# A decoder step on one core: work units dealt anew over the expert groups, ScalarE copies of the late projection, and column-group products in the samples' attention

## What is computed

```
h = x + W_out[ rms(NSA(n)) ; rms(ShortConv(n)) ],  n = rmsnorm(x)
h = h + PEER(rmsnorm(h))
y = h + sigmoid(rmsnorm(h) W_g) * (p W_p)
```

## Time and profile before

| | |
|---|---|
| median of 3 runs | 2665.53 us (2664.52 to 2675.07) |
| the profiled execution's own time | 2674.7 us |
| its span, first to last instruction | 2672.9 us |
| PE, DVE, POOL, ACT busy | 64%, 43%, 34%, 12% of the span |
| mean granted TensorE clock | 0.77 of full speed |
| moved by DMA | 907 MB, mean 339 GB/s |
| of it by the gathers' queue | 671 MB |

### The profile page before, as it was taken

One profiled execution on the slowest core, in us unless ns is written; L12 is line 12 of the kernel. 1 busy time (PEld: TensorE's weight loads), 2 busy tenths in 40 slices (PEclk: granted clock), 3 DMA queues, 4 the chain that ended last, 5 costly groups with the idle time before them and its releaser, 6 DMA issues.

```text
span 2672.9 us, 21406 instructions
## 1 busy us (share of the span) xinstructions
PE 1716.8 (64%) x8331; PEld 935.6 (35%) x8331; DVE 1147.8 (43%) x2124; ACT 331.3 (12%) x711; POOL 921.8 (34%) x644
## 2 busy tenths in 40 slices
PE   7599898998879467677678533332332323477776
PEld 3245576398767346543257300000000000122224
DVE  1001213105442773244543366656556665644442
ACT  1000123001000232120010010100101012001002
POOL 0000000003222452243343256656656655645430
PEclk9799896998889777678878766666565665777888
DMA  9673352768989797689899899999999999999996
GB/s 314 211 280 119 127 175 95 251 213 326 387 333 386 316 387 286 265 316 366 347 417 394 347 418 422 421 421 422 422 422 421 422 422 418 402 416 416 416 418 221
DMA packets 228650, 907.12 MB, mean 339 GB/s; under 512 B 29750, under 2 KB 54198, under 8 KB 144615
## 3 DMA queue, kind: packets, MB, share of 16 engines
q0 software_dynamic: 92160, 671.13, 60.9%
q1 hardware_dynamic: 136174, 233.79, 25.3%
q10 hardware_dynamic: 216, 0.86, 0.1%
HBM read 893.70 MB, written 14.52 MB: 340 GB/s over the span
## 4 chain that ended last, share of the span: by engine, by line
DMA 49%; PE 39%; DVE 4%; issue 2%; ACT 2%; POOL 2%; SPq 1%; DVEq 0%; ACTq 0%; PEldq 0%; POOLq 0%
DMA arena<-in_peer_v,arena 33%; PE bank L1660 8%; DMA arena<-in_w_in 6%; PE bank L2035 5%; PE bank L2052 4%; DMA arena<-in_w_out 3%; DMA arena<-in_peer_wq 3%; PE bank L1724 3%; DMA arena<-in_peer_u,arena 2%; PE bank L1852 2%; PE bank L1828 2%; PE bank L1985 2%; DVE arena L1457 2%; PE bank L2154 2%; DMA arena<-in_state_win 2%
## 5 line engine op out<-in xcount | busy, mean ns | idle before, releaser
L1457 DVE CUSTOM_DVE_ANT_0 arena<-arena 128x2048 f32<-128x2048 f32 x320 | 730.8, 2292 | 623.2 <-DMA arena<-in_peer_u,arena 619.7
L2035 PE MATMUL bank<-arena 128*32 128x512 f32 x2560 | 459.8, 830 | 673.8 <-DVE arena L1466 511.9
L658 POOL DMA_INDIRECT arena<-in_peer_u,arena x320 | 561.1, 1753 | 900.9 <-DVEq L1436 634.0
L663 POOL DMA_INDIRECT arena<-in_peer_v,arena x320 | 360.4, 1126 | 769.0 <-PE bank L2035 739.5
L2035 PEld LDWEIGHTS bank<-arena 128*32 128x32 f32 x2560 | 68.7, 128 | 1019.0 <-DVE arena L1466 516.8
L1660 PE MATMUL bank<-arena 128*128 128x512 f32 (+2 forms) x544 | 219.0, 563 | 37.8 <-DMA arena<-in_w_in 32.4
L2052 PE MATMUL bank<-arena 128*128 128x192 f32 x1024 | 193.4, 353 | 21.1 <-DMA arena<-in_w_in 19.7
L2052 PEld LDWEIGHTS bank<-arena 128*128 128x128 f32 x1024 | 184.9, 208 | 42.2 <-DMA arena<-in_w_in 25.2
L1660 PEld LDWEIGHTS bank<-arena 128*128 128x128 f32 (+1 forms) x544 | 102.7, 210 | 151.0 <-issue 117.6
L954 ACT ACTIVATE arena<-arena 128x4 f32<-128x4 f32 x80 | 16.7, 209 | 974.2 <-DVE arena L1457 974.1
L2154 PE MATMUL bank<-arena 128*128 128x512 f32 x256 | 120.2, 627 | 0.0
(11 more groups left out here) (245 smaller groups left out, 1528.1 us busy)
## 6 DMA issues: line engine op xcount, KB each, us to landing
arena<-in_w_in SPq DMA_DIRECT2D x22, 2048.0 KB, 13.3
arena<-in_w_in SPq DMA_DIRECT2D x32, 1024.0 KB, 14.6
arena<-in_w_out SPq DMA_DIRECT2D x8, 2048.0 KB, 8.2
arena<-in_peer_wq SPq DMA_DIRECT2D x8, 2048.0 KB, 8.0
arena<-in_w_out SPq DMA_DIRECT2D x16, 1024.0 KB, 16.3
arena<-in_peer_wq SPq DMA_DIRECT2D x16, 1024.0 KB, 22.9
arena<-in_ple_gate SPq DMA_DIRECT2D x32, 512.0 KB, 14.6
arena<-in_ple_gate SPq DMA_DIRECT2D x6, 2048.0 KB, 12.7
```

The costliest lines, as they stand in the source:

```text
L658: pool.indirect_dma_start(u_row[j], None, I["peer_u"][0], bass.IndirectOffsetOnAxis(idx[:, i, c + j:c + j + 1], 0)).then_inc(u_in[j], 16)
L663: pool.indirect_dma_start(v_row[j], None, I["peer_v"][0], bass.IndirectOffsetOnAxis(idx[:, i, c + j:c + j + 1], 0)).then_inc(v_in[j], 16)
L1457: dve.tensor_tensor_reduce(out=u_row[j], in0=u_row[j], in1=rep_of(i), scale=1.0, scalar=0.0, op0=ALU.mult, op1=ALU.add, accum_out=a4[:, pa ...
L2035: ins = pe.matmul(bank[i % 2][32 * q:32 * q + 32, :], diag[:, k % 2, j, :], v_row[j][:, 512 * q:512 * q + 512], start=(s == 0 and j == 0), ...
```

## The change

Four edits.

1. **Blocks h are copied like the others.** ScalarE's `late_out` copies h0 and h1 out of PSUM to a place that `h_hold` gives (for h0 the one that b1 uses later, so b1's copy waits for `ch_ev` 1). The next block waits for `cz_ev` alone. VectorE reads the copies. `late_conv` goes to groups 4 and 7, `conv_norm` to 8, `scale_conv` to 9, and ScalarE's and TensorE's parts with them; `conv_sums` is now at the start of group 8's items.
2. **The items are dealt anew**: groups 8, 9 and 10 take items 0-2, 3-5 and 6-8; groups 11 to 15 one each, 9 to 13; group 16 takes 14, 15 and 16; from 17 on as before.
3. **Score products of the samples** go round the four pairs: the same 28 products, each next one for another 32 partitions. `sample_scores(s)` no longer waits for the copy of the pair before last.
4. **Value products of the samples** keep 32 columns of probabilities stationary and stream 128 columns of values, round the same four groups of partitions of bank 3; ScalarE copies the 128x128 result (`sample_rows_out`), TensorE turns it once (`sample_turn`, behind the next pair's scores), and ScalarE copies it to its place. The next `value_load` waits for the products (`ov_mm`), not for the turn.

The diff, cut to its core:

```diff
@@ -173,6 +173,11 @@
     u_rows = buf(ZC0, 512)
+    def h_hold(j, x):
+        return (buf(Z0 + 3584, 4, 192)[:, x, 0:128], buf(Z0 + 3584, 4, 192)[:, x, 128:192]) if j else (conv_P(4 + x), conv_S(4 + x))
@@ -272,7 +277,9 @@
         if k < 8:
             return ()
-        return (2 * (k - 8), 2 * (k - 8) + 1) if k < 16 else (k,)
+        if k < 11:
+            return tuple(range(3 * (k - 8), 3 * (k - 8) + 3))
+        return (k - 2,) if k < 16 else (14, 15, 16) if k == 16 else (k,)
@@ -538,7 +545,10 @@
         def value_load(s):
-            sp.wait_ge(o_mm, 16 + s)
+            if s:
+                sp.wait_ge(ov_mm, s)
+            else:
+                sp.wait_ge(o_mm, 16)
@@ -844,11 +854,15 @@
+        def sample_rows_out(s):
+            act.wait_ge(ov_mm, s + 1)
+            act.activation(pT[:, 1, 0:128], bank[3][:, 0:128], ACT.Copy).then_inc(ov_ev, 1)
+
         def sample_o(s):
             act.wait_ge(o_mm, 16 + s + 1)
             for bb in range(2):
                 ins = act.activation(attT[:, :, (2 * s + bb) * NT:(2 * s + bb) * NT + NT],
-                                     bank[7][:, 384 + 64 * bb:448 + 64 * bb].rearrange("p (h t) -> p h t", h=NH), ACT.Copy)
+                                     bank[3][:, 128 + 64 * bb:192 + 64 * bb].rearrange("p (h t) -> p h t", h=NH), ACT.Copy)
@@ -886,9 +900,11 @@
             if 11 <= k < 15:
                 sample_pt(k - 11)
-                sample_o(k - 11)
+                sample_rows_out(k - 11)
             if 9 <= k < 13:
                 sample_keys(k - 9)
+            if 11 <= k < 15:
+                sample_o(k - 11)
@@ -969,9 +985,9 @@
             kind, j = LATE[b]
-            if kind == "h":
-                return
             act.wait_ge(rc_used, 4 * b + 4)
+            if kind == "b" and j:
+                act.wait_ge(ch_ev, 1)
@@ -985,9 +1001,10 @@
-                elif kind == "b":
-                    act.activation(conv_P(c), src_P, ACT.Copy)
-                    ins = act.activation(conv_S(c), src_S, ACT.Copy)
+                elif kind in "bh":
+                    dst_P, dst_S = h_hold(j, s) if kind == "h" else (conv_P(c), conv_S(c))
+                    act.activation(dst_P, src_P, ACT.Copy)
+                    ins = act.activation(dst_S, src_S, ACT.Copy)
@@ -1009,19 +1026,19 @@
-            if k == 4:
+            if k == 5:
                 u_rows_out(0)
             if k < 7:
                 late_out(k + 1)
-            if k == 6:
+            if k == 7:
                 act.wait_ge(cv_done, 2)
...
                 ins.then_inc(sqc_ready, 1)
-            if k == 7:
+                u_rows_out(1)
+            if k == 8:
                 root(stats[:, 244:246], stats[:, 246:248])
-                u_rows_out(1)
@@ -1532,14 +1549,14 @@
-            dve.wait_ge(cz_ev, 4 if j == 0 else 6)
+            dve.wait_ge(cz_ev, 5 if j == 0 else 8)
...
-            dve.wait_ge(rc_used, 20 if j == 0 else 32)
             for x in range(4):
-                for u, src in ((u_ext[:, x, 2:130], bank[4 + x][:, 0:128]),
-                               (by_sample(u_ext[:, x, 130:210], NT + 2)[:, :, 2:NT + 2], by_sample(bank[4 + x][:, 128:192], NT))):
+                h_P, h_S = h_hold(j, x)
+                for u, src in ((u_ext[:, x, 2:130], h_P),
+                               (by_sample(u_ext[:, x, 130:210], NT + 2)[:, :, 2:NT + 2], by_sample(h_S, NT))):
@@ -1577,8 +1594,8 @@
-        late = {1: head_norm, 2: lambda: scale_heads(0), 3: lambda: (scale_heads(1), late_conv(0)),
-                6: lambda: late_conv(1), 7: conv_norm, 8: scale_conv}
+        late = {1: head_norm, 2: lambda: scale_heads(0), 3: lambda: scale_heads(1), 4: lambda: late_conv(0),
+                7: lambda: late_conv(1), 8: conv_norm, 9: scale_conv}
@@ -1872,7 +1889,8 @@
-            pe.wait_ge(o_ev, 16 + max(0, s - 1))
+            if s == 0:
+                pe.wait_ge(o_ev, 16)
@@ -1883,20 +1901,20 @@
+            groups = [(2 * s + bb, bb, g, 64 * bb + 32 * g,
+                       qsT[:, 2 * s + bb, HPG * g:HPG * g + HPG, :].rearrange("p h t -> p (h t)")) for bb in range(2) for g in range(NG)]
+            for br in range(2):
+                for a in range(2):
+                    for b, bb, g, p0, q in groups:
+                        pe.matmul(bank[4 + br][p0:p0 + 32, 128 * a:128 * a + 128], q, pastT[:, bb, br, a, g, :],
+                                  start=True, stop=True)
...
@@ -1914,21 +1932,24 @@
-                r = slice(64 * bb + 32 * g, 64 * bb + 32 * g + 32)
-                    o = bank[7][:, 384 + r.start:384 + r.stop]
-                    for w in range(2):
-                        for k in range(2):
-                            pe.matmul(o, past_vals[:, w, bb, k, g * HD:g * HD + HD],
-                                      pT[:, 0, 256 * w + 128 * k + r.start:256 * w + 128 * k + r.stop],
-                                      start=(w == 0 and k == 0), stop=False)
...
-            ins.then_inc(o_mm, 1)
+            for w in range(2):
+                for k in range(2):
+                    for bb, g, r in groups:
+                        pe.matmul(bank[3][r, 0:HD], pT[:, 0, 256 * w + 128 * k + r.start:256 * w + 128 * k + r.stop],
+                                  past_vals[:, w, bb, k, g * HD:g * HD + HD], start=(w == 0 and k == 0), stop=False)
...
+            ins.then_inc(ov_mm, 1)
+
+        def sample_turn(s):
+            pe.wait_ge(ov_ev, s + 1)
+            pe.transpose(bank[3][:, 128:256], pT[:, 1, 0:128], ident).then_inc(o_mm, 1)
@@ -1997,6 +2018,8 @@
             if 9 <= k < 13:
                 sample_scores(k - 9)
+            if 11 <= k < 15:
+                sample_turn(k - 11)
@@ -2042,10 +2065,8 @@
-                elif LATE[b - 1][0] == "h":
-                    pe.wait_ge(ch_ev, LATE[b - 1][1] + 1)
                 else:
-                    pe.wait_ge(cz_ev, sum(kind != "h" for kind, _ in LATE[0:b]))
+                    pe.wait_ge(cz_ev, b)
@@ -2091,7 +2112,7 @@
-                4: lambda: u_turn(0), 7: lambda: (u_turn(1), conv_sums())}
+                5: lambda: u_turn(0)}
@@ -2106,6 +2127,9 @@
             if k == 8:
+                u_turn(1)
+                conv_sums()
+            if k == 9:
                 pe.wait_ge(roots_set, 2)
                 root_rows(bank[2], 0, 246, 247).then_inc(roots_mm, 1)
```

More of the change, by code:

```diff
@@ L232, in build @@
     rb_in = [sem(f"rb_in{j}") for j in range(4)]
-    half_ev = sem("half_ev")
+    half_ev, ov_mm, ov_ev = sem("half_ev"), sem("ov_mm"), sem("ov_ev")
     gs_mm = sem("gs_mm")
@@ L1049, in _ @@
                     spread_staged(k // SSTEP + 1)
-            if k < 8:
+            if k < 9:
                 late_behind(k)
@@ L1885, in sample_scores @@
             pe.wait_ge(biased, 16 + s)
-            for bb in range(2):
-                b = 2 * s + bb
-                for g in range(NG):
-                    p0 = 64 * bb + 32 * g
-                    q = qsT[:, b, HPG * g:HPG * g + HPG, :].rearrange("p h t -> p (h t)")
-                    for br in range(2):
-                        for a in range(2):
-                            pe.matmul(bank[4 + br][p0:p0 + 32, 128 * a:128 * a + 128], q, pastT[:, bb, br, a, g, :],
-                                      start=True, stop=True)
-                        pe.matmul(bank[4 + br][p0:p0 + 32, 256:264], q, qkT[:, 8 + 2 * br + g, 256 + b * NT:256 + b * NT + NT],
-                                  start=True, stop=True)
-                    sg = 2 * (1 + b) + g
-                    ins = pe.matmul(bank[4][p0:p0 + 32, 264:264 + NWIN], q, kcT[:, sg * NWIN:sg * NWIN + NWIN],
-                                    start=True, stop=True)
+            groups = [(2 * s + bb, bb, g, 64 * bb + 32 * g,
[4 more added lines that the diff above has]
+                        pe.matmul(bank[4 + br][p0:p0 + 32, 128 * a:128 * a + 128], q, pastT[:, bb, br, a, g, :],
+                                  start=True, stop=True)
+                for b, bb, g, p0, q in groups:
+                    pe.matmul(bank[4 + br][p0:p0 + 32, 256:264], q, qkT[:, 8 + 2 * br + g, 256 + b * NT:256 + b * NT + NT],
+                              start=True, stop=True)
+            for b, bb, g, p0, q in groups:
+                sg = 2 * (1 + b) + g
+                ins = pe.matmul(bank[4][p0:p0 + 32, 264:264 + NWIN], q, kcT[:, sg * NWIN:sg * NWIN + NWIN],
+                                start=True, stop=True)
             ins.then_inc(s_mm, 1)
```

14 lines of the change are left out of this document (7 added, 7 removed).

## The result

The changed kernel took **2629.74 us** (median of 4 runs, 2622.26 to 2634.76), the kernel before, beside it, 2667.73 us: ratio 0.9851, interval 0.9819 to 0.9884. So it is 1.5 to 1.7% faster, 38 to 47 us; forecast were 62, in a range that holds the result.

A forecast was written before the change was run, and what follows sets the result against it. The DMA engines bound the kernel, full from group 28; only their earlier idle time can be won. Gains of 22 (groups 0-7) and 40 (groups 8-16) make 62 us off the median 2665.5: 2603.5, rounded 2604, range 2584 to 2634.

The forecast's parts named there:

- Groups 0-7: First stage: copying blocks h by ScalarE removes nearly both DMA holes, gaining 22 of 24.5 us idle, range 12 to 24.5.
- nothing to speak of: Groups 0-7: cost of eight added ScalarE copies per block, 2 us, which TensorE waits for instead of VectorE's products.
- Groups 8-10: Three items each: 13.4 us more on VectorE make 77 us, about 16 idle, where 63.6 and 5.0 were.
- Groups 11-16: One item a group is hidden behind the gathers; of 51.1 us idle, 3 remain, in group 16.
- the loads' wait: Groups 11-16: with one item a group, the wait for a samples' load still left is 9 us.
- Groups 17 on: From group 17 to the end: the same work, so a change of 0.
- 5 either way: Groups 17 on: a late start of the projection's weights could give 5 us either way.
- The loads aren't hidden: Rival, groups 14, 15 and 16: the 9 us waits come out whole, 27 us less gain, 2631 us; chance 0.15.
- The column groups don't overlap: Rival, samples' products: value products take 6.2 to 12 us per pair, still within the 26 covered; 2607 us; chance 0.05.
- All is hidden: Rival, groups 8-10: VectorE's three items fit beside the gathers, 2586 us; chance 0.17.
- Denser VectorE slows the gathers' descriptors: Rival, groups with three items: v gathers take 2.2 us each, 15 us in all, 2619 us; chance 0.15.
- Slower: Rival, six groups after 8-10: each a serial loop of 45 us, above 39.5 decides; +46, 2711 us; chance 0.03.

The follow-up runs named there:

- e1: The kernel before with only ScalarE's copies of blocks h and the moves that go with them: 2654.23 us, ratio 0.9920 to the kernel before.
- e3: The changed kernel with the items dealt as in the kernel before: 2629.83 us, ratio 0.9827 to the kernel before.
- e5: The changed kernel run again unaltered, as the control (its second trace): 2631.18 us, ratio 0.9828 to the kernel before.
- e9: The changed kernel with three items in group 8, two each in 9 to 12, one each in 13 to 15, three in 16: 2619.85 us, ratio 0.9801.
- e7: The changed kernel with the samples' score and value products issued pair after pair instead of round the four column groups: 2640.74 us, ratio 0.9855.
- e10: Like e9, but items 13 and 14 in group 15, and 15 and 16 in group 16: 2633.68 us, ratio 0.9851 to the kernel before.
- e6: The changed kernel with SP's loads of p moved behind the output projection's weights 2 to 18: 2633.24 us, ratio 0.9827 to the kernel before.

## Why the prediction was right, and where not

**The sign and the mechanisms** were right: 38 to 47 us for 62. In idle time the forecast was 103.3 - 62 = 41 left of the stretch; measured were 55 and 63. By its own steps:

- *Groups 0-7, forecast 22.* The waits of 27 and 29 us of VectorE's late_conv are gone (line 1560 has no idle time before it). The length fell by 22.0, e1 alone measures 21 to 22; but in idle time it is 14.5 us in the first trace and 19.6 in the second, and the rest of the length is transfers that moved to later stages. The hole that stayed is in group 7:

```profile
854.90:864.90 10.00, 8.34 (x36) 8.12 (x40) 1.28 (x2) 0.00 (x0) 0.00 (x0) 0.66 0.49 203
```

The timeline tells how it arises, first of ScalarE, then of VectorE:

```profile
864.91 0.28 ACT L1006 ACTIVATE arena<-bank 128x128 f32<-128x128 f32 x1 [31.32 <-PE bank L2073]
...
865.96 0.28 ACT L970 ACTIVATE arena<-arena 128x4 f32<-128x4 f32 x1
...
866.34 0.16 DVE L1481 TENSOR_TENSOR arena<-arena 128x4 f32<-128x4 f32 x1 [10.17 <-ACT arena L970]
```

  ScalarE waits 31.3 us for block h1's last quarter, with the gelu of group 7 behind that wait; VectorE, its products done at 856.1, waits 10.2 us for the gelu, and the weighted rows and the v gathers behind it. The forecast had put the new copies at "nothing to speak of" and looked only at TensorE, which waits for them. What the forecast missed is the queue on the new engine: **the wait was moved from VectorE to ScalarE, not removed.** VectorE's wait for this gelu stands in e1 (9.0 us), e3 (10.3), e5 (8.9) and e9 (13.0) too. Whether the copy would be better behind the gelu was not tried.
- *Groups 8-10, forecast 77 us and 16 idle.* 80.7 and 82.0 us, 15.2 and 14.6 idle. The idle time is right; the length has 7 to 9 us of transfers more than before. But the reason given was not right. The forecast added 13.4 us of VectorE work; VectorE's busy time rose by 6.6 (52.3 to 58.9 us), and its share of the stage fell from 82% to 73%. In the middle group (31.0 us at a share of 0.67) it is busy 21.5. What grew is the waiting between engines within the items: VectorE waits 11.0 us for TensorE's scores (line 1792) for 5.1 before, and the v gathers wait 34.1 us for TensorE for 19.1.
- *Groups 11-16, forecast 162 us and 3 of idle.* 161.7 us, but by luck: 9.6 idle, and 12 us of transfers gone elsewhere. The value products came in as forecast: 3.1 us that ScalarE waits for a pair (12.4 us in four waits), for 13.7 before; going round is 6.9/128 = 54 ns of busy time each in e5, at a mean granted clock of 0.69. The term that was short is the loads' wait, "9 us". Waits from 915 to 1105 us, and two of the three landings in the chain:

```profile
POOL arena L673 <- PE bank L2058: 92.0, 15, 24.6
...
PE bank L1899 <- DMA arena<-in_state_win: 31.7, 2, 21.6
...
PE bank L1929 <- DMA arena<-in_state_win: 28.1, 2, 17.9
```

```profile
1006.44 28.54 DMA arena<-in_state_win
...
1059.64 24.16 DMA arena<-in_state_win
```

  The landing that the forecast took as 18.5 us is 24 to 29, so TensorE waits 18 and 22 us instead of 9. It isn't that the engines are full only now: in the 18.5 us their share was 0.99, in the two landings shown 1.03 and 1.02. But 7.3 MB were moved then, and 11.5 and 9.9 MB now, so more transfers stood beside the load. That this is the cause wasn't tested. After the first of the two landings, 8.9 us of idle time show from 1034.9 to 1054.9 (share 0.56). And the groups are not 22 to 25 us each but uneven, 16 to 39: the one at 978.40 is 32.9 us long at a share of 1.03, with no idle time at all: 13.5 MB are moved in it, keys and values among them, where a group's gathers are 8.
- *Groups 17 on, forecast "the same work; 0".* **This is the step that failed.** 20.4 us more: 15.2 of transfers that came in from the stages before, and 5.2 of idle time. Group 18 alone is 51.4 us for 27.7, and TensorE does more in it, 40.9 us of busy time for 17.7: item 17's work has slipped into it, behind weights that came late. It waits 13.1 us for weights in it (10.0 before), and 6.7 us of idle time follow from 1164.9 on. The forecast stated the principle ("the bytes stay the same, so a stage gains what it loses of idle time") and then took 223.6 us of full engines for groups 8-16 as if these bytes were tied to their stage. They are tied to the items, and the items were dealt anew. The "5 either way" that it allowed for late weights is the size of the idle time, 5.2. It had named "if groups 17-27 get longer" as a sign of being wrong, and they did, from 338.9 to 359.5 us. Another of its signs, TensorE's waits for loads holding POOL back in groups 13-16, came in part: POOL's longest wait for TensorE is 24.6 us, 33.1 before.
- *The sum.* Counted in idle time, the first trace has 22 us more than the forecast left: 7.5 in groups 0-7, 9.4 in 8-16 and 5.2 from 17 on. The second has 14: 2.4, 6.9 and 5.1. So the step "0" is by far the largest miss in length, but a quarter to a third of the miss in idle time; most of its 20.4 us are transfers whose departure had been counted as a gain further up. And the sum priced each edit in the kernel before. Alone, the deal is worth 17 us and the products 31; beside the products and the copies the deal is worth nothing measurable, for the two reasons given above.
- *Rivals.* "The loads aren't hidden", at 2631, is nearest in its time and in part in its mechanism (TensorE's waits of 18 to 22 us), though it wanted 27 us more in groups 14 to 16, where 2 us are idle, 9.6 in all of groups 11-16. "The column groups don't overlap": refuted by e7, which measures their worth at 10 us (forecast 3). "All is hidden" is refuted by the 15 us of idle time in groups 8-10. "Denser VectorE slows the gathers' descriptors": in groups 8-10 one u gather took 1416 ns for 1574 before, one v gather 1619 for 1503, POOL's busy time 31.0 us for 33.6, so no cost of 15 us. But VectorE had not become denser there (73% busy for 82%), so this tests the rival's price and not its rule. The shared port of the Trainium skill's page SBUF — State Buffer, section "SBUF: two separate sides", shows no added cost here; whether it costs anything, no run shows. "Slower" wanted six groups above 39.5 us; the longest was 39.2, the others 16 to 33.

## What to carry over

Where transfers bound a stretch, count the idle time of their engines over the whole of it, up to the point from which the kernel runs alike again; a stage's length also changes by transfers that have only moved, and a lengthened group need not cost anything. Edits that fill the same idle time don't add up, and an edit that costs little while its neighbours have idle time can cost more once they are full: try each alone and each left out before the last one is kept. A copy given to another engine takes its wait along: look at what is queued behind it there.

## What the runs showed of the hardware

Products whose output takes 32 partitions run beside one another in four column groups if they are issued in turn (54 ns of busy time each, e5) and far less so if not (211 ns, e7), with the same 350 ns for each in the trace: the mean duration of one doesn't show it, only the busy time of the group does. A load of the samples took 24 to 29 us to land, for 18.5 before, with the engines full in both (1.02 to 1.03, and 0.99): a full share doesn't tell how long a landing takes. And issuing itself can stand: the timeline of SP in the changed kernel, two of the output weights and the loads of p behind them,

```profile
1107.33 1.14 SPq L574 DMA_DIRECT2D arena<-in_w_out  x2
1108.65 11.44 SPq L366 DMA_DIRECT2D arena<-in_p_prompt  x2
1120.13 4.03 SPq L367 DMA_DIRECT2D arena<-in_p_sample  x1
```

has 0.57 us for an issue and right behind it 5.7 us (mean of two) and 4.0. The same three loads of p took 15.5 us to issue here, 14.8 in e5 and 5.5 in e9, but 2.2 in e3, 2.0 before and 1.3 in e10. In e5 and here the engines' share was 1.01 to 1.02, but it was 1.04 in e3 as well, so the share doesn't tell them apart. What holds SP there wasn't tested; e6, without these loads in that place, took the control's time within 3 us.
